# Decode attention with zero-padded queries held stationary and the window caches fetched a stage earlier

## The reference, cut to what matters

```
s = einsum('bqgjd,bngd->bgjqn', qg, kc) * scale          # compressed keys, 127 of them
p = masked_softmax(s, ...);  o_cmp = p @ vc
imp = p @ overlap_matrix;    idx = top_k(imp, 16)        # blocks of 64 keys
s = qg @ keys[idx] * scale;  o_slc = masked_softmax(s) @ values[idx]    # 2048 cached keys and the new one
s = qg @ kw * scale;         o_win = masked_softmax(s) @ vw             # window of 512
o = g0 * o_cmp + g1 * o_slc + g2 * o_win
```

## Time and profile before

| | us |
|---|---|
| median of 3 runs | 2595.2 (2590.91 to 2596.66) |
| the profiled execution's own time | 2594.46 |
| its span, first to last instruction | 2592.7 |
| PE busy | 2248.4 (87% of the span) |
| DVE busy | 1060.4 (41%) |
| ACT busy | 572.1 (22%) |
| POOL busy | 452.3 (17%) |
| mean granted TensorE clock | 0.914 of full speed |
| DMA, mean over the span | 63 GB/s, 164.57 MB |

### The profile page before, as it was taken

How to read it: one execution, slowest core, us unless ns; L and a number is a source line. 1 busy time by engine, 2 the same in 40 slices (tenths; PEclk the granted TensorE clock), 3 DMA queues, 4 the chain that set the end, 5 groups by cost and what they waited for, 6 DMA issues and landing times. The chain is left out here.

```text
span 2592.7 us, 32982 instructions
## 1 busy us (share of the span) xinstructions
PE 2248.4 (87%) x13162; PEld 1915.6 (74%) x13162; DVE 1060.4 (41%) x1988; ACT 572.1 (22%) x1010; POOL 452.3 (17%) x174
## 2 busy tenths in 40 slices
PE   5598896899978689787599999888999999998997
PEld 3487685333338559787588887878998989898996
DVE  1755064556632304444511111316543434444345
ACT  2476164334331101111101101112111110110110
POOL 0202010134441011111010110212222221121120
PEclk9799898899986589889799999898999999999998
DMA  7111153000013141111123231311111111111101
GB/s 272 54 45 56 35 194 136 1 1 1 1 65 119 49 138 33 42 50 51 49 83 92 79 113 34 113 43 52 42 48 50 46 37 50 34 49 50 33 33 67
DMA packets 135814, 164.57 MB, mean 63 GB/s; under 512 B 11058, under 2 KB 108083, under 8 KB 131108
## 3 DMA queue, kind: packets, MB, share of 16 engines
q1 hardware_dynamic: 125366, 109.85, 14.0%
q0 software_dynamic: 7552, 48.16, 5.5%
q10 hardware_dynamic: 2768, 4.70, 0.5%
HBM read 149.10 MB, written 17.87 MB: 64 GB/s over the span
## 5 line engine op out<-in xcount | busy, mean ns | idle before, releaser
L242 PE MATMUL psall<-hT,ring_short 128*128 128x344 f32 x1536 | 505.0, 329 | 63.4 <-POOL ring_short L237 40.8
L244 PE MATMUL psall<-hT,ring_short 128*128 128x344 f32 x1536 | 497.9, 324 | 0.0
L243 PE MATMUL psall<-work_short,ring_short 128*128 128x344 f32 x1296 | 419.5, 324 | 15.1 <-issue 15.1
L237 POOL TENSOR_TENSOR ring_short<-ring,ring_short 128x2048 fp32r<-128x2048 f32 (+3 forms) x49 | 197.8, 4037 | 1026.3 <-DVE ring_short L232 1026.3
L242 PEld LDWEIGHTS psall<-hT,ring_short 128*128 128x128 f32 x1536 | 295.8, 193 | 66.0 <-issue 36.3
L244 PEld LDWEIGHTS psall<-hT,ring_short 128*128 128x128 f32 x1536 | 295.8, 193 | 15.7 <-issue 15.7
L243 PEld LDWEIGHTS psall<-work_short,ring_short 128*128 128x128 f32 x1296 | 247.9, 191 | 0.6
L2656 DVE SCALAR_TENSOR_TENSOR xT<-psall,mod,xT 128x344 f32<-128x344 f32 (+1 forms) x264 | 151.4, 573 | 129.5 <-PE psall L244 126.4
L242 PE MATMUL psall<-work_short,work_short 128*128 128x344 f32 x480 | 160.9, 335 | 0.0
L243 PE MATMUL psall<-xT_short,ring_short 128*128 128x344 f32 x480 | 158.2, 330 | 0.0
L1090 POOL TENSOR_TENSOR ring<-ring 128x1024 f32<-128x1024 f32 x50 | 120.2, 2405 | 206.4 <-ACT ring L1233 154.3
(11 more groups left out here) (382 smaller groups left out, 4043.7 us busy)
## 6 DMA issues: line engine op xcount, KB each, us to landing
ring<-in_ada_w SPq DMA_DIRECT2D x24, 1024.0 KB, 6.5
ring<-in_w_up SPq DMA_DIRECT2D x44, 512.0 KB, 5.0
ring<-in_w_in SPq DMA_DIRECT2D x20, 512.0 KB, 4.0
work<-in_w_down SPq DMA_DIRECT2D x10, 1024.0 KB, 4.9
x_spill<-xT SPq DMA_DIRECT2D x1, 4128.0 KB, 17.3
xT<-x_spill SPq DMA_DIRECT2D x1, 4128.0 KB, 14.7
work<-in_x_prompt ACTq DMA_DIRECT2D x1, 4096.0 KB
work<-in_w_in SPq DMA_DIRECT2D x8, 512.0 KB, 5.3
```

What stands on the lines that cost most here:

```text
L237: return eng.tensor_tensor(lo, src, hi, ALU.subtract)
L242: pe.matmul(out, w[0], x[0], start=first, stop=False)
L243: pe.matmul(out, w[0], x[1], start=False, stop=False)
L244: return pe.matmul(out, w[1], x[0], start=False, stop=last)
```

## The change

- Window keys (8 loads) and the window values of sequences 0 to 3 (4 loads) are issued by SP in the prompt attention stage, into the places of the split keys and queries, and that stage's SP waits for them. The values of sequences 4 to 7 are loaded in the decode stage once all window keys are turned.
- The four ring buffers are then free from the start: keys of four sequences are gathered at once.
- Scores: the weights are now the queries, 64 columns that are zero but for the 8 of the sequence (`qpad`), and the turned keys are the moving side, 256 (window) or 512 columns at a time. The sum over the 8 sequences is accumulated in PSUM, so that the rows (8 sequences by 8 heads) come out as rows. Half of the keys go to output partitions 0 to 63 and half to 64 to 127, by two products on the two halves of the array's columns. A row of scores is now 128 partitions by 1024 columns. The transposes to rows and the score copies go.
- Because a softmax row now lies on two partitions 64 apart, maximum and sum are exchanged between the halves by small products on PE (`swap`), twice for each of the two softmaxes.
- `select` moves into the loop, behind the key copies of sequence 6.
- Values: weights of 32 columns, of which 8 are used, to output partitions 32k to 32k+31, in the four quarters k; the quarters are summed at the end by a product with `fold`. The window values come before the gathered ones.

```diff
+def window_home(b):
+    return 8256 + 1032 * (b // 2) + 512 * (b % 2)
+def value_home(b):
+    return 12384 + 1032 * (b // 2) + 512 * (b % 2) if b < 4 else 9356 + 512 * (b - 4)
...
             sp.dma_start(hot, T["c_hot"]).then_inc(masks_in, 16)
+            sp.wait_ge(k_split, 3)
+            for b in range(4):
+                sp.dma_start(view(s.work, value_home(b), 4, P),
+                             T["cache_win_v"][0, b].rearrange("(p t) g d -> p t (g d)", t=4)).then_inc(fetched, 16)
+            sp.wait_ge(q_split, TT)
+            for b in range(NB):
+                sp.dma_start(view(s.work, window_home(b), 4, P),
+                             T["cache_win_k"][0, b].rearrange("(p t) g d -> p t (g d)", t=4)).then_inc(fetched, 16)
+            sp.wait_ge(fetched, 16 * (NB + 4))
...
-                if b >= 2:
-                    pool.wait_ge(turned, 4 * (b - 1))
+                if b >= BUFS:
+                    pool.wait_ge(turned, NB + 4 * (b - BUFS + 1))
                 gather(T["cache_slc_k"], b)
...
-            def dots(keys, n, b, slot):
-                for k in range(n):
-                    last = pe.matmul(s.ps[5 + slot % 2][:, k * NH:(k + 1) * NH], keys[:, k, :],
-                                     qbd[:, b * NH:(b + 1) * NH], start=True, stop=True)
+            def window_dots(b):
+                pe.wait_ge(evac_a if b % 2 else evac_v, b // 2 + 1)
+                for i, half in enumerate(HALVES):
+                    last = pe.matmul(S_win[half], qpad[:, b, :], win_keysT[b][:, 2 * i:2 * i + 2, :], start=(b == 0),
+                                     stop=(b == NB - 1))
...
+            def dots(b):
+                pe.wait_ge(evac_v, NB // 2 + 2 * b + 2)
+                pe.wait_ge(evac_a, NB // 2 + 2 * b + 2)
+                for y in range(2):
+                    for i, half in enumerate(HALVES):
+                        c = 2 * y + i
+                        last = pe.matmul(S[half, 512 * y:512 * (y + 1)], qpad[:, b, :],
+                                         keysT[b % 2][:, 4 * c:4 * c + 4, :], start=(b == 0), stop=(b == NB - 1))
                 last.then_inc(dotted, 1)
...
+            def swap(column, at):
+                v_done()
+                for i, half in enumerate(HALVES):
+                    last = pe.matmul(misc[half, at:at + 1], s.ident[:, HALVES[1 - i]], st[:, column:column + 1],
+                                     start=True, stop=True)
+                signal(last)
...
             pe.wait_ge(q_ready, 1)
             for b in range(NB):
-                if b >= 4:
-                    pe.wait_ge(evac_a if b % 2 else evac_v, (b - 4) // 2 + 1)
-                turn_keys(win_keys[b], 1, b)
+                turn_window(b)
+                if b == 1:
+                    compressed_scores()
+                if b >= 2:
+                    window_dots(b - 2)
+            window_dots(NB - 2)
+            window_dots(NB - 1)
+            turn_keys(0)
             for b in range(NB):
                 if b + 1 < NB:
+                    turn_keys(b + 1)
+                dots(b)
                 if b < len(steps):
                     steps[b]()
-            pe.wait_ge(dots_read, 2 * NB)
-            v_done()
-            to_rows(scT, 16, s.ps[0:4])
-            v_done()
-            to_keys(16, s.ps[0:2], 0)
             v_done()
+            swap(5, 320)
+            swap(6, 321)
+            turn_rows(rows, 8, s.ps[2:4])
+            v_done()
...
             for b in range(NB):
-                pe.wait_ge(buf_in[of[b]], 16 * (b // BUFS + 3))
-                for k in range(16):
-                    last = pe.matmul(O[:, b, :], head(prT[:, k, :], b), buf[of[b]][:, k, :], start=False, stop=False,
-                                     skip_group_check=True)
+                pe.wait_ge(buf_in[b % BUFS], 16 * (b // BUFS + 3))
+                for y in range(2):
+                    for i in range(2):
+                        for k in range(4):
+                            last = pe.matmul(O[quad(k), b, :], weights(prT, 4 * y + k, i, b),
+                                             buf[b % BUFS][:, 4 * (2 * y + i) + k, :], start=False,
+                                             stop=(b % 4 == 3 and y + i == 2), skip_group_check=True)
                 last.then_inc(vals_used, 1)
-            pe.wait_ge(wv_in, 16 * NB)
...
             for b in range(NB):
-                last = pe.transpose(s.ps[5][:, b * NH:(b + 1) * NH], o_rows[:, b, :], s.ident[0:NH, 0:NH])
+                last = pe.matmul(s.ps[4][:, b * NH:(b + 1) * NH], o_rows[:, b, :], s.fold[:, 0:NH], start=True, stop=True)
...
-            steps = (compressed_rows, compressed_weights, importance, window_rows, window_weights)
+            steps = (compressed_rows, compressed_weights, importance, exponents, lambda: scale(win_rows, 2),
+                     window_weights, select)
+            v.memset(qpad, 0.0)
             ch.link(v, v.memset(qbd, 0.0))
...
+            for b in range(NB):
+                v.tensor_copy(qpad[:, b, b * NH:(b + 1) * NH], qbd[:, b * NH:(b + 1) * NH])
...
-            ch.link(v, v.tensor_tensor(blocks(rows), blocks(s.psall[0:ROWS, 0:2048]),
-                                       bc(pen[:, 0:32].unsqueeze(1).unsqueeze(3), (ROWS, 16, 32, 4)), ALU.add))
-            softmax(2048, 1)
+            v.wait_ge(dotted, NB)
+            ch.link(v, v.tensor_tensor(blocks(rows), blocks(S), bc(pen[:, 0:32].unsqueeze(1).unsqueeze(3), (P, 8, 32, 4)),
+                                       ALU.add))
+            top(rows, 3)
+            exponents()
+            scale(rows, 1)
```

More of the change, by code:

```diff
@@ L1367, in stage_decode_attention @@
[L1367 to L1387, removed]
+    win_keys = [view(s.work, window_home(b), 4, P) for b in range(NB)]
+    win_vals = [view(s.work, value_home(b), 4, P) for b in range(NB)]
@@ new lines, in stage_decode_attention @@
+    keysT = [view(s.work, X3 + 2048 * i, 16, P) for i in range(2)]
+    win_keysT = [view(s.work, X3 + 512 * b, 4, P) for b in range(NB)]
+    rows = view(s.work, 23880, 1024)
+    prT = view(s.work, 24904, 8 * P + 32)
+    win_prT = view(s.work, 25960, 2 * P + 32)
+    o_rows = view(s.work, 23880, NB, P)
+    lower, eq, gt = view(s.work, 14448, NS_S * NS_S), view(s.work, 8256, NS_S * NS_S), view(s.work, 23880, NS_S * NS_S)
+    Z = 15544
+    qpad = view(s.work, Z, NB, ROWS)
+    qbd = view(s.work, Z + 512, ROWS)
@@ new lines, in stage_decode_attention @@
+    knew = view(s.work, Z + 576, 2, NB)
+    gate = view(s.work, Z + 592, 3)
+    own = view(s.work, Z + 596, NB)
+    over = view(s.work, Z + 604, NS_S)
+    st = view(s.work, Z + 640, 16)
+    imp = view(s.work, Z + 656, NS_S)
+    grp = view(s.work, Z + 692, NB * NG)
+    pen = view(s.work, Z + 708, NS_S)
+    new_d = view(s.work, Z + 744, NB)
+    cmp_sc = view(s.work, Z + 752, 2, ROWS)
+    L = 11404
+    cmp_rows = view(s.work, L, P)
+    grp_all = view(s.work, L + 128, 2, ROWS)
+    cmp_pT = view(s.work, L + 256, P)
@@ L1447, in v_done, with turn_window @@
                 pe.wait_ge(v_to_pe, from_v[0])
-            def turn_keys(src, chunks, first):
-                for c in range(chunks):
+            def turn_window(b):
+                if b >= 4:
+                    pe.wait_ge(evac_a if b % 2 else evac_v, (b - 4) // 2 + 1)
+                for k in range(4):
+                    last = pe.transpose(s.ps[b % 4][:, k * P:(k + 1) * P], win_keys[b][:, k, :], s.ident[:, :])
+                last.then_inc(turned, 1)
+            def window_dots(b):
[3 more added lines that the diff above has]
+                                     stop=(b == NB - 1))
+                if b == NB - 1:
+                    last.then_inc(win_dotted, 1)
@@ L1451, in turn_keys @@
+            def turn_keys(b):
+                pe.wait_ge(buf_in[b % BUFS], 16 * (b // BUFS + 1))
+                for c in range(4):
+                    pe.wait_ge(evac_a if c % 2 else evac_v, NB // 2 + 2 * (b - 1) + c // 2 + 1)
                     for k in range(4):
-                        last = pe.transpose(s.ps[(first + c) % 4][:, k * P:(k + 1) * P], src[:, 4 * c + k, :], s.ident[:, :])
+                        last = pe.transpose(s.ps[c][:, k * P:(k + 1) * P], buf[b % BUFS][:, 4 * c + k, :], s.ident[:, :])
@@ L1556, in _ @@
-            pe.wait_ge(wv_in, 16 * NB)
-            for b in range(NB):
-                for k in range(4):
-                    last = pe.matmul(O[:, b, :], head(win_prT[:, k, :], b), win_vals[b][:, k, :], start=False,
-                                     stop=(b % 4 == 3 and k == 3), skip_group_check=True)
-            signal(last)
+                if b == 4:
+                    pe.wait_ge(values_in, 16 * 4)
+                for k in (3, 0, 1, 2):
+                    pe.matmul(O[quad(k), b, :], weights(win_prT, k % 2, k // 2, b), win_vals[b][:, k, :],
+                              start=first and k == 3, stop=False, skip_group_check=True)
```

236 lines of the change are left out of this document (111 added, 125 removed).

## The result

The changed kernel takes 2505.66 us (median of 4 runs, 2500.32 to 2512.97) against 2595.93 for the kernel before; the ratio is 0.9658, 95% interval 0.9635 to 0.9681. That is 90 us less between the medians and 88 in the profiled pair, where the prediction had 71 and the range began at 2507. The profiled execution has a span of 2504.5 us.

What follows compares the result with a forecast made beforehand. It took the decode stage as one chain of about 192 us, each microsecond saved coming off the total. Loop 42.6, behind it 8.5, values 21.4, less 1.3 at the end: 71.2 us less, 2524 us; range 2507 to 2550.

Steps and rivals of the forecast that it cites:

- window part: Start of decode stage: window key transposes, compressed products and eight pairs of score products, from 766.9 to 781.0 us.
- loop: Decode loop over sequences: clock a quarter of the way from high (52.8 us) to low (73.4), so 58 us, to 841.2.
- end: After the last value product: 2.4 us as before, plus 1.3 for summing the quarters with 16 records of about 0.12.
- rival 2: Clock rises early and transfers keep up: loop -5 us, values -4.5, start -3; total 2511, chance 0.14.
- The price of a pair: Score products on two PSUM halves: 0.86 us per further pair, 0.15 for leaving the form; 1.87 per sequence at high clock.
- rivals 3 and 4: 3: change of form dearer or no overlap, +34, 2558, chance 0.07; 4: each column-part change drains the array, 2605, 0.02.
- rival 5: Window loads don't come early, because the prompt stage waits or they push something: 14 us return, 2538, chance 0.04.
- early loads: Window key loads issued in the prompt stage cost nothing, with 79 us of cover before PE's first decode product.
- link (a): Start of the old decode stage: PE does 3.6 us of compressed products, then waits for window keys; 14 us at stake.
- Rival 1: Clock stays low in the loop and at its start: loop +15.4 us, start +5, values +4; 2548, chance 0.18.
- selection: Inside the loop ahead of sequence 7's copies: 9.0 us from turning 7 to its products, of which PE covers 4.1 or 7.3.
- The quarters' step: Value products: only neighbours of different quarters overlap, so 0.116 us each at high clock; bounds 0.231 and 0.058.

Runs made afterwards that it cites:

- E1: Changed kernel with score products of one half, and gathered value products of one quarter, issued next to each other; decode stage 123.2 us against 122.8.
- E3: Changed kernel with the 12 window key and value loads issued at the start of the decode stage, PE waiting for them; stage 143.2 us, 20.4 longer.
- E4: Changed kernel with the selection moved back behind the loop on VectorE; decode stage 118.4 us, 4.4 shorter.
- E5: Changed kernel with small value products issued by kind instead of sequence by sequence; that part 10.5 us against 12.5, decode stage 120.1 against 122.8.
- second pair: Kernel before and changed kernel, both unchanged, each profiled once more; decode stage 195.9 and 124.5 us, nine MLP passes 655.1 and 630.0.
- E10: Changed kernel, unchanged, profiled once more; decode stage 124.5 us, nine MLP passes 630.0 us with two stops.

## Why the prediction was right where it was, and which step failed

| link | forecast | measured |
|---|---|---|
| window part, PE's first product to the first gathered keys | 14.1 | 15.5 |
| turning sequence 0, loop, last score products | 60.2 | 56.3 |
| behind the loop | 12.0 | 11.5 |
| small and window values | 9.5 | 12.5 |
| gathered values | 19.5 | 19.6 |
| end | 3.7 | 5.4 |
| sum | 119.0 | 120.8 |

The sum is nearer than its terms. The links missed by +1.4, -3.9, -0.5, +3.0, +0.1 and +1.7 us, and that these add up to 1.8 is luck. Of the rivals, only the loop of rival 2 came nearly as it said (5 us shorter); neither its start nor its values did. The price of a pair stands against rivals 3 and 4, the first transposes right behind the query block against rival 5.

- **The price of a pair** was right to the hundredth: 1.87 us for two pairs and the change of form. Leaving the form costs what the earlier trace rows had, and E1 shows that the order within it is free. The Trainium skill's rule that a change of tiling mode drains the engine (TensorEngine Tiling, Key Properties) shows in the loop as no more than that 0.15 us.
- **The window part** was 1.4 us longer. Three rounds of transposes and a pair ran at the low clock, not two (769.36 to 775.46, 2.03 each against the 1.77 assumed), and the forecast left out the change of form that it had priced for `dots`. Its last term is also added up wrongly: four transposes of 0.56 and six pairs of 0.43 are 4.8, not 5.1.
- **The early loads** cost the prompt stage nothing that shows (it ended at 762.8 us with them and 763.3 without them in E3), and the wait of 10.6 us is gone. E3 shows 20.4 us for loading late in the changed kernel, not the 14 of link (a), and it moves more than the keys.
- **The loop** was 3.9 us shorter than forecast. VectorE's waits were 14.4 us against the 15 taken over. The clock was nearer to the high level than the quarter of the way that I assumed: a mean of 0.92. Rival 1 is out. The Trainium skill's sentence that transposes don't bring the full clock (TensorE: Matmul & The Clock Gate, Part 4) had the earlier trace rows against it, 0.90 under transposes alone; the loop, half of it transposes, doesn't bear it out either, though it can't test it alone.
- **The selection** took 8.6 us from turning 7 to its products (823.89 to 832.48), forecast 9.0. But the forecast took its place as given and didn't see that it adds a wait of VectorE for PE; E4 is 4.4 us shorter.
- **The quarters' step failed.** "PE keeps its order, so that ... only neighbours of different quarters" overlap is wrong: at the low clock 32 window products took 3.41 us (E5), 0.107 each and a quarter of the 0.44 of one alone; that is four at once, the lower bound that I had set aside. At the high clock a gathered one took 0.068 (868.59), where the forecast had 0.116. It didn't show in the sum for two reasons that cancel or cover: the gathers end the gathered link, as forecast (19.6 against 19.5), and the small products, forecast at 9.5 us for a mixed clock, ran wholly at the low one; for that case the forecast had 13.7, measured are 12.5.
- **The end** was mis-sized by 1.7 us: the 16 records of `fold` ran at the low clock (3.58 us).
- **The step that failed by size** is the one that isn't in the sum. The prediction took "Every microsecond taken out of that chain comes off the total", and nothing else, and it had no term for stages with the same code. Outside the stage the profiled pair differs by 17.8 us. Of it 14.3 is the MLP loop, by fewer stops of PE and the low clock behind them (in the second pair 25.1, at 655.1 against 630.0); the rest is within the scatter of executions. Rows of the kernel before showed those stops; I hadn't looked past the stage, and the trace of before alone would not have said that they would go.

## What to carry to other kernels

Products with few columns of weights gain by the number of array parts that they are spread over, as long as those for one part aren't issued in a long row (four were too many here); count the busiest part, not the products, and count it for each kind of product by itself. When PE gets faster in a link fed by transfers, issue first what frees the buffers: here that order alone was worth 13.7 us of a stage of 122.8. And profile both kernels twice before putting a change in total down to the edited stage.

## What the runs showed of the hardware that was not expected

- Four products on four quarters of the output partitions run at once at the price of one (0.43 us for four at the low clock, E5), also with each in two records.
- The same program position in the MLP loop has PE standing still for 2.3 to 4.2 us with nothing in the profile that it waits for, and the granted clock behind such a stop is about 0.5 for some 3 us, so that in the changed kernel's first profile a pass with one stop of 2.4 to 3.3 us took 4.3 to 5.1 us longer. Once, in E10, it didn't fall (stop of 2.4 us, pass 2.6 longer). An edit of a stage hundreds of microseconds earlier took away one of two such stops in all of its variants, and 200 idle instructions did not move either.
- Products of 127 and of 8 rows of weights for different quarters did not overlap (0.57 us apart at the low clock), while products of one kind did.
- Of the same part, 8, 16 and 32 products took 3.55, 3.56 and 3.41 us, as they used one, two or four quarters.
